# The down projection of a fused two-block kernel, rewritten as seven products of half blocks for each pair of tiles

## The reference

```python
h = rmsnorm(x, ffn_norm[l])
gu = h @ w_gate_up[l]
gt, up = jnp.split(gu, 2, axis=-1)
x = x + (jax.nn.silu(gt) * up) @ w_down[l]
return rmsnorm(x, final_norm)
```

## Time and profile before

| what | value |
|---|---|
| median of 3 runs | 3848.51 us (3847.26 to 3848.73) |
| the profiled execution | 3840.01 us, its span 3838.2 us |
| TensorE busy | 3710.5 us, 97% of the span |
| VectorE, ScalarE, GpSimd busy | 1644.0, 1280.1, 872.9 us |
| down projection, 3672.76 to 3823.83 | 151.07 us |
| gate and up, tiles 1 to 21, 3418.94 to 3672.76 | 253.82 us |

### The profile page before, as it was taken

How to read it: one execution, slowest core, us unless ns; L and a number is a source line. 1 busy time by engine, 2 the same in 40 slices (tenths; PEclk the granted TensorE clock), 3 DMA queues, 4 the chain that set the end, 5 groups by cost and what they waited for, 6 DMA issues and landing times.

```text
span 3838.2 us, 51758 instructions
## 1 busy us (share of the span) xinstructions
PE 3710.5 (97%) x21538; PEld 2208.8 (58%) x21538; DVE 1644.0 (43%) x2963; ACT 1280.1 (33%) x2375; POOL 872.9 (23%) x888
## 2 busy tenths in 40 slices
PE   7999999999999999999999999999999999999998
PEld 3565555655555545677666664444455544458853
DVE  1433432233322110777777771355677741134411
ACT  3444443222222012444444441476454421010000
POOL 0000000101100000666666661122454420000000
PEclk9999999999999999999999999999999999999999
DMA  5111002010102112110111011122110111212221
GB/s 211 53 64 72 31 23 88 23 66 6 60 33 88 60 44 88 45 41 30 43 45 45 29 67 50 65 82 72 45 46 18 43 56 61 107 66 88 81 76 52
DMA packets 24249, 226.49 MB, mean 59 GB/s; under 512 B 2640, under 2 KB 5200, under 8 KB 8784
## 3 DMA queue, kind: packets, MB, share of 16 engines
q1 hardware_dynamic: 24016, 223.18, 15.7%
HBM read 221.07 MB, written 2.10 MB: 58 GB/s over the span
## 4 chain that ended last, share of the span: by engine, by line
PE 91%; DVE 4%; ACT 1%; DMA 1%; issue 1%; POOL 1%; DVEq 0%; SPq 0%; POOLq 0%; ACTq 0%
PE bank L1195 9%; PE bank L1526 7%; PE bank L1142 6%; PE bank L1205 5%; PE bank L956 4%; PE bank L1053 4%; PE bank L909 4%; PE bank L1537 4%; PE bank L1318 3%; PE bank L1185 3%; PE bank L895 3%; PE bank L1078 2%; PE bank L975 2%; PE bank L1277 2%; PE bank L1109 2%; PE bank L1457 2%
## 5 line engine op out<-in xcount | busy, mean ns | idle before, releaser
L1195 PE MATMUL bank<-hT,ring 128*128 128x256 f32 (+1 forms) x1024 | 349.8, 490 | 0.0
L1195 PEld LDWEIGHTS bank<-hT,ring 128*128 128x128 f32 x1024 | 189.6, 190 | 122.0 <-issue 108.1
L1142 PE MATMUL bank<-Y,ring 128*128 128x512 f32 (+1 forms) x704 | 247.8, 515 | 0.0
L1142 PEld LDWEIGHTS bank<-Y,ring 128*128 128x128 f32 x704 | 133.8, 190 | 113.8 <-issue 107.1
L956 PE MATMUL bank<-hT,ring 128*128 128x256 f32 (+1 forms) x512 | 186.5, 501 | 2.4 <-ACT hT L1612 2.4
L1318 PE MATMUL bank<-hT,ring 128*128 128x512 f32 x384 | 178.9, 599 | 4.7 <-ACT Y L1618 4.7
L909 PE MATMUL bank<-hT,ring 128*128 128x256 f32 (+1 forms) x512 | 182.3, 493 | 0.0
L1205 PE MATMUL bank<-ring,hT 128*128 128x128 f32 x1536 | 182.0, 277 | 0.0
L1205 PEld LDWEIGHTS bank<-ring,hT 128*128 128x128 f32 x1536 | 176.3, 192 | 2.1
L1053 PE MATMUL bank<-hT,ring 128*128 128x256 f32 (+1 forms) x512 | 171.8, 486 | 0.0
L1596 ACT ACTIVATE arena<-xT 128x512 f32<-128x512 f32 (+1 forms) x40 | 23.5, 587 | 437.4 <-DVE xT L2329 237.8
(11 more groups left out here) (437 smaller groups left out, 7140.1 us busy)
## 6 DMA issues: line engine op xcount, KB each, us to landing
ring<-in_w SPq DMA_DIRECT2D x60, 2048.0 KB, 7.8
ring<-in_w SPq DMA_DIRECT2D x17, 1536.0 KB, 6.7
ring<-in_w SPq DMA_DIRECT2D x20, 1280.0 KB, 5.5
ring<-in_w SPq DMA_DIRECT2D x12, 1024.0 KB, 4.8
ring<-in_w SPq DMA_DIRECT2D x8, 1408.0 KB, 5.9
ring<-in_w SPq DMA_DIRECT2D x19, 512.0 KB, 3.3
xT<-in_xT SPq DMA_DIRECT2D x1, 3072.0 KB, 11.7
out<-arena SPq DMA_DIRECT2D x8, 256.0 KB, 2.3
```

The costliest lines, as they stand in the source:

```text
L1142: ins = e.matmul(m[:, 0:b - a], w[:, k, sl(j % 2)], src[:, k, a:b], start=k == 0, stop=k == kt - 1)
L1195: ins = e.matmul(m[:, 0:b - a], w[:, k, sl(1 + d)], hT[:, k, a:b], start=k == 0, stop=k == 7)
```

## The change

Down is done in four pairs of output tiles, p = 0 to 3, each a 2x2 block problem like a tile of gate and up: output tiles 2p and 2p + 1, the contraction in two halves of 11 blocks, the positions in two halves, in seven products of 11 matmuls of 256 columns. In the order of TensorE (banks a, b, c, d): 0 a; 1 b; 2 d; 3 c; 4 onto a; 5 onto d; 6 onto c.

- A slab now holds both tiles of a pair over half the contraction; a pair opens two slabs of the same size as before. The lower one is released by product 2, the upper one by product 6.
- The sums of activations (`down_T`) are made in `gu_p` behind the product: one of 256 columns for each of the inner tiles 0 to 10, three for each of 11 to 21. They go to free places in `xT`, `hT`, `Y` and the arena.
- The sums of weights (`down_s(p, 0)` to `(p, 3)`, S1 to S4) are four operations of 1408 elements. For p = 0 two stand ahead of `gu_p(21)` and two behind it; for later pairs three stand in the middle of the pair before and the fourth at its end.
- ScalarE copies the first partial sum (`down_p1`); VectorE has seven operations a pair in place of two additions.
- `norm_pairs` takes the place of `norm_tiles(4, ...)`: squares and running sums go by pairs, and the running sum of tile 6 comes behind the last pair.
- The output tiles `of` move from the arena into `hT`, and the norm's scratch moves too.

```diff
+def norm_pairs(n, name):
+    made = []
+    for p in range(4):
+        made += [("nx", n, 0, j) for j in (2 * p - 2, 2 * p - 1) if j > 0]
+        made += [(name, p), ("nq", n, 0, 2 * p), ("nq", n, 0, 2 * p + 1)]
+    return made + [("nx", n, 0, 6), ("nm", n, 0, 0), ("nm", n, 1, 0)]
...
-    return made + [("gu_p", 21)]
+    return made + [("down_s", 0, 0), ("down_s", 0, 1), ("gu_p", 21), ("down_s", 0, 2), ("down_s", 0, 3)]
...
-         + [("tables",)] + norm_tiles(4, "down") + norm_rest(4) + [("out",)])
+         + [("tables",)] + norm_pairs(4, "down") + norm_rest(4) + [("out",)])
...
-    "wo": lambda j: ["wo"] * (j % 4 == 0), "gu": lambda j: ["gu"] * (j % 2 == 0), "down": lambda j: ["down"],
+    "wo": lambda j: ["wo"] * (j % 4 == 0), "gu": lambda j: ["gu"] * (j % 2 == 0), "down": lambda p: ["down", "down"],
...
-    "gu_vec": ("gu_prod", "gu_s", "gu_t", "gu_u"),
-    "gu_act": ("gu_p1", "gu_silu"),
+    "gu_vec": ("gu_prod", "gu_s", "gu_t", "gu_u", "down_s", "down_t", "down_u"),
+    "gu_act": ("gu_p1", "gu_silu", "down_p1"),
...
-        of = arena_[:, 0:4096].rearrange("p (k t) -> p k t", k=8)
+        of = hT_[:, :].rearrange("p (k t) -> p k t", k=8)[:, :, 0:LAT]
...
-            a = 0 if n < 3 else 8192
+            a = 0 if n < 3 else 8192 if n == 3 else 4096
...
+        spots = ([xT[:, i, LAT:ALL] for i in range(8)] + free_h + [Y_[:, 11264 + 256 * i:11520 + 256 * i] for i in range(12)]
+                 + [arena_[:, 8192 + 256 * i:8448 + 256 * i] for i in range(5)])
+        down_T = [spots[0:11], spots[11:22], [yf[:, n, HALF[1]] for n in range(11)], spots[22:33]]
+        down_S = [arena_[:, a:a + 1408].rearrange("p (k c) -> p k c", k=11) for a in (9472, 0, 2048, 11264)]
+        down_1, down_2, down_g = (arena_[:, 12800 + 256 * i:13056 + 256 * i] for i in range(3))
+        down_u = arena_[:, 13568:14080]
+        def down_factors(p):
+            lo, hi = (ring[:, i % NRING * SLOT:i % NRING * SLOT + 2816].rearrange("p (k n) -> p k n", k=11)
+                      for i in (spot["down_slab", p], spot["down_slab", p] + 1))
+            return lo[:, :, sl(1)], hi[:, :, sl(1)], lo[:, :, sl(0)], hi[:, :, sl(0)]
...
-            def down(j):
-                w = slab("down", 22)
-                m = take(proj, ("down", j), ("down_x", j))
-                for k in range(22):
-                    if j == 0:
-                        q.wait_ge(*on("gu_prod", k))
-                    ins = e.matmul(m, w[:, k, :], yf[:, k, :], start=k == 0, stop=k == 21)
-                ins.then_inc(up("down_mm", j), 1)
-                give("down", "down_mm", j)
+            def down(p):
+                slab("down", 11)
+                spot["down_slab", p] = open_w["down"][1]
+                slab("down", 11)
+                g_lo, g_hi, u_lo, u_hi = down_factors(p)
+                (h1, h2), (t1, t2, t3, t4), (s1, s2, s3, s4) = HALF, down_T, down_S
+                a, b, c, d = (take(4 * (p % 2) + n, ("down", p, n), ("down_u", (p, i)))[:, 0:256] for n, i in enumerate((3, 0, 5, 4)))
+                for n, (m, l, r, first) in enumerate((
+                        (a, g_lo, [yf[:, k, h1] for k in range(11)], True), (b, s2, t2, True), (d, s3, t3, True), (c, s1, t1, True),
+                        (a, g_hi, [yf[:, k, h1] for k in range(11, 22)], False), (d, u_hi, t4, False),
+                        (c, s4, [yf[:, k, h2] for k in range(11, 22)], False))):
+                    if n in (1, 2, 3, 6):
+                        q.wait_ge(*on("down_s", (p, {1: 1, 2: 2, 3: 0, 6: 3}[n])))
+                    elif n:
+                        q.wait_ge(*(on("down_p1", p) if n == 4 else on("down_u", (p, 1))))
+                    if n == 6:
+                        q.wait_ge(*on("down_u", (p, 2)))
+                    for k in range(11):
+                        if p == 0 and n in (0, 4, 6):
+                            q.wait_ge(*on("gu_prod", k if n == 0 else 11 + k))
+                        elif p == 0:
+                            q.wait_ge(*on("down_t", ({1: 1, 2: 2, 3: 0, 5: 3}[n], k)))
+                        ins = e.matmul(m, l[:, k], r[k], start=first and k == 0, stop=k == 10, skip_group_check=True)
+                    ins.then_inc(up("down_mm", (p, n)), 1)
+                spot["slab", spot["down_slab", p]] = ("down_mm", (p, 2))
+                marks.gives.setdefault(now[0], []).append(spot["down_slab", p])
+                give("down", "down_mm", (p, 6))
...
+            def down(p):
+                q.wait_ge(*on("down_mm", (p, 0)))
+                if p:
+                    q.wait_ge(*on("down_u", (p - 1, 0)))
+                e.activation(down_1, bank[spot["down", p, 0]][:, 0:256], ACT.Copy).then_inc(up("down_p1", p), 1)
...
                     q.wait_ge(*on("gu_u", (j, 3)))
                 e.tensor_tensor(yf[:, j, :], yf[:, j, :], gu_up[j % 2] if j else bank[spot["gu", 0, 1]],
                                 ALU.mult).then_inc(up("gu_prod", j), 1)
+                q.wait_ge(*on("gu_prod", j))
+                (h1, h2), k, (t1, t2, t3, t4) = HALF, j % 11, (t[j % 11] for t in down_T)
+                if j < 11:
+                    if j == 0:
+                        q.wait_ge(*on("wo_mm", 7))
+                    e.tensor_tensor(t1, yf[:, j, h2], yf[:, j, h1], ALU.subtract).then_inc(up("down_t", (0, k)), 1)
+                    return
+                q.wait_ge(*on("down_t", (0, k)))
+                e.tensor_tensor(t2, yf[:, j, h2], t1, ALU.subtract).then_inc(up("down_t", (1, k)), 1)
+                e.tensor_tensor(t3, yf[:, j, h2], t3, ALU.subtract).then_inc(up("down_t", (2, k)), 1)
+                q.wait_ge(*on("down_t", (1, k)))
+                e.tensor_tensor(t4, yf[:, j, h1], t2, ALU.subtract).then_inc(up("down_t", (3, k)), 1)
...
-            def down(j):
-                q.wait_ge(*on("down_mm", j))
-                e.tensor_tensor(xT[:, j, 0:LAT], bank[spot["down", j]], xT[:, j, 0:LAT], ALU.add).then_inc(up("down_x", j), 1)
+            def down_s(p, n):
+                g_lo, g_hi, u_lo, u_hi = down_factors(p)
+                i = spot["down_slab", p]
+                l, r, op = ((u_lo, u_hi, ALU.add), (down_S[0], g_lo, ALU.subtract), (g_lo, u_lo, ALU.subtract),
+                            (g_hi, down_S[1], ALU.subtract))[n]
+                for a in (i, i + 1):
+                    q.wait_ge(*on(f"w{a % NRING}", a))
+                if p:
+                    q.wait_ge(*on("down_mm", (p - 1, (3, 1, 2, 6)[n])))
+                elif n:
+                    q.wait_ge(*on("gu_mm", (20 if n == 1 else 21, 6)))
+                if n in (1, 3):
+                    q.wait_ge(*on("down_s", (p, n // 2)))
+                if p == 0 and n == 3:
+                    q.wait_ge(*on("gu_prod", 21))
+                e.tensor_tensor(down_S[n], l, r, op).then_inc(up("down_s", (p, n)), 1)
+            def down(p):
+                a, b, c, d = (bank[spot["down", p, n]][:, 0:256] for n in range(4))
+                (h1, h2), (u1, u2), x, x1 = HALF, (down_u[:, h] for h in HALF), xT[:, 2 * p, 0:LAT], xT[:, 2 * p + 1, 0:LAT]
+                q.wait_ge(*on("down_p1", p))
+                q.wait_ge(*on("down_mm", (p, 1)))
+                if p:
+                    q.wait_ge(*on("down_x", 2 * p - 1))
+                else:
+                    q.wait_ge(*on("gu_prod", 21))
+                e.tensor_tensor(down_2, b, down_1, ALU.add).then_inc(up("down_u", (p, 0)), 1)
+                q.wait_ge(*on("down_u", (p, 0)))
+                q.wait_ge(*on("down_mm", (p, 2)))
+                e.tensor_tensor(u2, d, down_2, ALU.add).then_inc(up("down_u", (p, 1)), 1)
+                q.wait_ge(*on("down_u", (p, 1)))
+                q.wait_ge(*on("down_mm", (p, 3)))
+                e.tensor_tensor(u2, c, u2, ALU.add).then_inc(up("down_u", (p, 2)), 1)
+                if p < 3:
+                    for n in range(3):
+                        down_s(p + 1, n)
+                q.wait_ge(*on("down_mm", (p, 4)))
+                e.tensor_tensor(x1[:, h1], a, x1[:, h1], ALU.add).then_inc(up("down_u", (p, 3)), 1)
+                q.wait_ge(*on("down_mm", (p, 5)))
+                e.tensor_tensor(u1, d, down_2, ALU.add).then_inc(up("down_u", (p, 4)), 1)
+                q.wait_ge(*on("down_u", (p, 4)))
+                e.tensor_tensor(x, down_u, x, ALU.add).then_inc(up("down_x", 2 * p), 1)
+                q.wait_ge(*on("down_mm", (p, 6)))
+                e.tensor_tensor(down_g, c, down_2, ALU.add).then_inc(up("down_u", (p, 5)), 1)
+                q.wait_ge(*on("down_u", (p, 5)))
+                e.tensor_tensor(x1[:, h2], down_g, x1[:, h2], ALU.add).then_inc(up("down_x", 2 * p + 1), 1)
+                if p < 3:
+                    down_s(p + 1, 3)
...
-    W += [slab(g["w_down_2"][0], (128 * j, 128 * j + 128)) for j in range(8)]
+    for p in range(4):
+        w = slab(g["w_down_2"][0], (256 * p, 256 * p + 256))
+        W += [w[:, 0:2816], w[:, 2816:5632]]
```

(4 more changed lines are left out.)

## The result

| | before | after |
|---|---|---|
| median of the first comparison | 3847.89 us (4 runs) | 3823.39 us (4 runs, 3820.60 to 3830.86) |
| ratio, 95% interval | | 0.9943 [0.9925, 0.9961] |
| the profiled execution, its span | 3840.01, 3838.2 us | 3824.72, 3822.9 us |
| median of all runs of the study | 3845.5 us (76 runs, 3839.9 to 3852.9) | 3826.8 us (19 runs, 3820.6 to 3835.0) |

One more run of the kernel before, 4882.72 us in a slower state, is left out of the 76.

What follows compares the result with a forecast made beforehand. The prediction took TensorE, busy for 97% of the span, as the bound. Products -18.1 us, covered work 0 and the end +1.0 us gave -17.1 us, so 3848.5 - 17.1 = 3831.4 us, range 3827 to 3839.

Steps and rivals of the forecast that it cites:

- The products: Down's matmuls: 352 instructions in 151.07 us become 616 of 256 columns in 132.95 us, gaining 18.1 us.
- The weight loads: Down on TensorE: 264 more loads of 0.19 us each lie under the matmuls, costing nothing; about 99 us if uncovered.
- The sums of activations: VectorE in gate and up: 44 operations of 256 columns fit its idle time, cost 0; 19 us without cover.
- the sums of weights: VectorE at down's first pair: four operations, 1.62 us each, covered by TensorE's first product; cost 0, bounds 0 and 1 us.
- the slabs: Down's weight transfers: eight slabs, 5.9 us each from issue to landing, arrive with 13 us slack; cost 0.
- the later pairs: VectorE's sums within down's pairs after the first finish before TensorE needs them; cost 0, bounds 0 and 1 us per pair.
- The end: From down's last product to ScalarE going on: longer additions, an exposed norm sum and matmul cost 1.0 us, bounds 0.2 and 1.4.
- The output stage: After the final norm: same work from another place in SBUF, cost 0, bounds -0.5 and +0.5 us.
- The sum: Whole kernel: -18.1 + 0 + 1.0 = -17.1 us, span 3821.1 us, median 3831.4 us, ratio 0.9956.
- the pace: Rival in down: 256-column spacing of 0.2158 us does not hold, slower beyond 0.256 us, 3948 with loads open; chance 0.03.
- the sums out of cover: Rival in down's first pair: VectorE's weight sums 2.5 times slower, 9 us lost, time 3840; chance 0.05.
- The slab ring: Rival in down: upper slab free only at pair end, 5.9 us waits at three pair starts, 17.7 us, time 3849; chance 0.04.

Runs made afterwards that it cites:

- eighth: Changed kernel with product 0 of each down pair made twice, so eight products per pair; 3845.8 us, ratio 1.000 to the kernel before.
- ring_late: Changed kernel with each pair's lower slab released by its last product instead of product 2; 3849.12 us, ratio 1.0012 to the kernel before.
- sums_behind: Changed kernel with all four first-pair weight sums behind gate and up's last VectorE product, instead of two ahead; 3827.59 us, ratio 0.9949 to before.
- fillers: Changed kernel plus 5 or 6 unread matmuls in each of three TensorE idles behind norms; 3825.76 us, or 3824.00 us with the direct third norm matmul too.
- tail_direct: Changed kernel without the final norm's last running sum, tile 6's square going directly into a third norm matmul; 3829.19 us, ratio 0.9952 to before.

## Why the prediction was right or wrong

*The products*: 132.95 us forecast, 132.97 measured; right, the spacing of 0.2158 holds for groups of 22 on a bank as for groups of 8, and in `eighth` for groups of 44.

*The weight loads*: hidden, as the gate and up stage had said; 116.85 us of loads in 132.95 us. The rule of the Trainium skill that a load overlaps a running matmul only when its row group differs ("TensorE: Matmul & The Clock Gate", "The mechanism" of Part 3) doesn't fit this trace either: loads and matmuls here share all rows. The same section also lets a load into a background weight buffer go ahead, which the prediction left out; whether that is what happens here, no run shows. The 99 us that the prediction gives for loads in the open compare an open new stage with a covered old one. Open in both, the old stage would be 352 x (0.4292 + 0.19) = 218 us, and the loss 32 us.

*The sums of activations, the sums of weights, the slabs, the later pairs*: no wait of TensorE in the stage, and the times read above are within 0.5 us of what was worked out.

*The end*: +1.06 us, forecast +1.0.

*The output stage*: forecast 0, with -0.5 as its lower bound. From the root's start to the end it was 11.60 us (3826.60 to 3838.2) and is 10.95 (3811.95 to 3822.9), -0.65. The first of VectorE's five scalings, before and after:

```profile
3828.05 1.85 DVE arena L2114
```

```profile
3813.33 0.75 DVE hT L2161
```

It is 1.1 us shorter, though all five together take 6.42 us instead of 6.50 and GpSimd's three products 5.10 instead of 4.59. So the first store is issued 2.16 us behind the root instead of 3.33. The issues end at 8.66 us instead of 8.95 (0.29 of the 0.65 us), and the last store lands 2.29 us behind them instead of 2.65 (0.36). What ties this to the new place of `of` was not tried and stays open.

*The sum*: -18.1 + 1.06 - 0.65 = -17.7 us, forecast -17.1. The forecast span for the profiled execution was 3821.1 us; it came out as 3822.9, because its first part and middle were 2.4 us longer than in the trace of before.

*The step that failed* is the one from the trace to the median: "3848.5 - 17.1 = **3831.4 us**", with "about 1 us of the spread of the runs". The 3848.5 was a median of three runs. With 76 runs it is 3845.5 us, and single runs span 13 us. The 8.0 us come from four parts:

- The first three runs lay in the upper half, which put the base 3.0 us too high.
- The four of the first comparison have a median 3.4 us under the changed kernel's median of 19; that is chance, with single runs that span 14 us.
- The term itself was 0.6 us short, nearly all of it in the output stage, which had been put at nothing.
- About 1 us is left between the medians' distance (18.7) and the trace's (17.7), inside its error.

The profiled execution of before, at 3840.01 us, was the warning: it was 7 us below the lowest of the three runs shown. I read the distance as a fixed ratio between profiled and timed runs, and it was spread: in the twelve later runs the profiled execution lies anywhere from 4.2 us below its median to 7.1 above it. The four executions known at that time have a mean of 3846.1 us and a standard deviation of 4.1. From these, 3846.1 - 17.1 = 3829.0 us would have been the forecast, and two medians of four runs with that spread are uncertain against each other by about 6 us either way (an estimate). That gives 3823 to 3835 before any stall is counted. The forecast ratio of 0.9956 was near: all runs give 3826.8 / 3845.5 = 0.9951.

*The rivals*: the pace and the sums out of cover did not come. The slab ring was priced at 17.7 us and was more: from gate and up's first matmul to the end the trace of `ring_late` took 3854.5 - 3410.0 = 444.5 us against 418.2, which is 26.3 more, of it 18.3 us of waits and 7.5 of slower clock; by the medians it is 22.3.

## What to carry to other kernels

A stage that is bound by TensorE without gaps can be priced closely from a stage of the same kernel that already has the new form (here 132.95 us forecast and 132.97 measured); then only the covers have to be worked out, each against the one operation that is wanted next. Before a range for a median is given, compare the profiled execution with the runs beside it: if they differ by more than the runs do among themselves, the spread is larger than the runs show, and it belongs into the range. A wait of TensorE can cost more than its length, by the slower clock behind it: 2.0 to 3.1 us more behind the 6 us waits of `ring_late`, nothing to be seen behind the 1.3 us wait of `sums_behind`.

## What the runs showed of the hardware

- The program's spread of 10 us and more comes nearly all from ahead of its last part (436 us before, 418 after). In the seven traces of the two kernels the last part repeats to 0.1 or 0.2 us, while the middle takes 2188.3 us or 2191.0 to 2191.7.
- The same idle of TensorE can be followed by a lower granted clock in one execution and not in another, and places differ in how often. In the first profile of the changed kernel, behind an idle of 2.70 us, the granted clock of 1384 to 1394 us is 0.83; in the profile of before that stretch is at 1.00 behind the same idle. Over the twelve traces without fillers the clock fell there in five, at the second norm's place (2417 to 2426 us, idle 2.4 us) in all twelve, for 1.7 us each, and ahead of gate and up (idle 2.4 us) in eleven, for 2.8 us in ten of them (1.2 in `tail_direct`; not in `eighth`).
- Behind an idle of 6 us TensorE lost 2.0 to 3.1 us more, at three of three places in the one trace of `ring_late`.
- VectorE's f32 operations on two tensors take 0.42, 0.69, 1.22 and 1.62 us for 256, 512, 1024 and 1408 elements in these last stages, where GpSimd is idle: one line, with about 0.15 us at its foot.
